# Expert 14's share of expert 15's rows: a product on TensorE in place of a scatter and a gather

## The reference, cut to what matters

```python
def ec_moe(h, router_w, w_gate, w_up, w_down):
    cap = EC_CAPACITY_FACTOR * t // N_EXPERTS          # 2 * 1024 // 16 = 128
    aff = softmax(h @ router_w)
    gate, idx = lax.top_k(swapaxes(aff, 1, 2), cap)     # each expert takes its 128 best tokens
    xs = h[bidx, idx]
    hid = silu(xs @ w_gate) * (xs @ w_up)
    ye = (hid @ w_down) * gate[..., None]
    return zeros_like(h).at[bidx, idx].add(ye)
...
y_lat = ec_moe(h_lat, ...)
x = x + mod_lat[5] * rms_norm(y_lat, norm_g[l, 3])      # the output
```

## Time and profile before

| | us |
|---|---|
| median of three runs | 1482.08 |
| the profiled execution | 1480.8 |
| its span, first to last instruction | 1479.0 |
| TensorE busy | 1302.7 (88%) |
| VectorE busy | 762.0 (52%) |
| ScalarE busy | 479.0 (32%) |
| GpSimd busy | 232.4 (16%) |
| mean granted TensorE clock | 0.948 |

### The profile page before, as it was taken

One profiled execution on the slowest core, in us unless ns is written; L12 is line 12 of the kernel. 1 busy time (PEld: TensorE's weight loads), 2 busy tenths in 40 slices (PEclk: granted clock), 3 DMA queues, 4 the chain that ended last, 5 costly groups with the idle time before them and its releaser, 6 DMA issues.

```text
span 1479.0 us, 13899 instructions
## 1 busy us (share of the span) xinstructions
PE 1302.7 (88%) x5053; PEld 757.3 (51%) x5053; DVE 762.0 (52%) x1079; ACT 479.0 (32%) x1115; POOL 232.4 (16%) x207
## 2 busy tenths in 40 slices
PE   6898998989999999889999969997079999999971
PEld 1444454445545555589989834454034444444430
DVE  1238888978893667577777745563900011001041
ACT  1723542561311222556667623343011110110140
POOL 0001320221000000155554300000010110110121
PEclk9899999999999999999999989998579999999985
DMA  8511544425315110256665654433659999999876
GB/s 305 173 29 50 172 150 143 130 79 180 101 42 157 29 29 20 57 164 172 188 190 188 198 204 154 152 140 109 256 173 356 325 337 341 332 329 337 295 223 147
DMA packets 175274, 264.63 MB, mean 179 GB/s; under 512 B 49069, under 2 KB 91814, under 8 KB 175206
## 3 DMA queue, kind: packets, MB, share of 16 engines
q1 hardware_dynamic: 151286, 204.32, 41.6%
q0 software_dynamic: 14416, 52.96, 12.1%
q10 hardware_dynamic: 9504, 6.45, 1.4%
HBM read 214.47 MB, written 49.22 MB: 178 GB/s over the span
## 4 chain that ended last, share of the span: by engine, by line
PE 59%; DMA 13%; ACT 10%; DVE 10%; issue 4%; SPq 1%; POOL 1%; POOLq 0%; DVEq 0%; ACTq 0%
PE ps L1737 26%; PE ps L1062 12%; PE ps L1081 6%; DMA arena<-g_dram 5%; DMA y_dram<-arena 3%; DMA arena<-zt_dram 2%; PE ps L1026 2%; ACT arena L512 2%; PE ps L1634 2%; PE ps L375 2%; ACT arena L521 1%; PE ps L1688 1%; DVE arena L2046 1%; PE ps L1658 1%; DVE arena L568 1%
## 5 line engine op out<-in xcount | busy, mean ns | idle before, releaser
L1737 PE MATMUL ps<-arena 128*128 128x512 f32 (+1 forms) x1120 | 444.7, 553 | 0.0
L1737 PEld LDWEIGHTS ps<-arena 128*128 128x128 f32 x1120 | 211.9, 192 | 208.5 <-issue 203.3
L1062 PE MATMUL ps<-arena 128*128 128x512 f32 x512 | 228.0, 599 | 1.4 <-ACT arena L1178 1.4
L2046 DVE SCALAR_TENSOR_TENSOR arena<-arena,taps 128x1024 f32<-128x1024 f32 x160 | 213.5, 1334 | 5.7
L1062 PEld LDWEIGHTS ps<-arena 128*128 128x128 f32 x512 | 97.2, 193 | 117.3 <-issue 115.3
L375 PE MATMUL ps<-arena 128*128 128x128 f32 x1080 | 133.7, 279 | 19.1 <-DVE arena L592 15.8
L375 PEld LDWEIGHTS ps<-arena 128*128 128x128 f32 x1080 | 128.9, 193 | 25.6 <-DVE arena L592 19.1
L1341 DVE TENSOR_TENSOR arena<-arena,ps 128x512 f32<-128x512 f32 x16 | 11.0, 687 | 213.4 <-PE ps L1062 213.4
L1026 PE MATMUL ps<-arena 128*128 128x512 f32 x256 | 116.3, 610 | 4.6 <-ACT arena L1127 4.6
L1081 PE MATMUL ps<-arena 128*128 128x512 f32 x256 | 115.6, 606 | 4.9 <-DVE arena L1351 4.9
L1026 PEld LDWEIGHTS ps<-arena 128*128 128x128 f32 x256 | 48.7, 195 | 62.7 <-issue 56.2
(11 more groups left out here) (287 smaller groups left out, 1621.5 us busy)
## 6 DMA issues: line engine op xcount, KB each, us to landing
arena<-exp_w_gate SPq DMA_DIRECT2D x16, 2048.0 KB, 11.3
arena<-exp_w_up SPq DMA_DIRECT2D x16, 2048.0 KB, 8.9
arena<-exp_w_down SPq DMA_DIRECT2D x16, 2048.0 KB, 11.1
arena<-ada_w POOLq DMA_DIRECT2D x16, 1024.0 KB, 6.6
arena<-w_in SPq DMA_DIRECT2D x28, 512.0 KB, 4.0
arena<-ada_w SPq DMA_DIRECT2D x4, 2048.0 KB, 10.6
arena<-x SPq DMA_DIRECT2D x16, 512.0 KB, 8.9
arena<-g_dram SPq DMA_DIRECT2D x16, 512.0 KB, 4.6
```

Source lines behind the costliest of these rows:

```text
L1062: last = mm(ps[gu_bank[s] + j][:], xsT[s][:, k, :], ew[s][j][:, k, :], start=(k == 0), stop=(k == KD - 1))
L1737: last = mm(ps[3 * (m % 2) + gi][:, 0:w], wring[(m + 1) % NW][:, k, :], hT[:, k, o:o + w], start=(k == 0), stop=(k == KD - 1))
L2046: ins = v.scalar_tensor_tensor(accg, cin_l[ci % 2][:, j // 3:j // 3 + GR, j % 3:j % 3 + GW], tp[:, j:j + 1], accg, ALU.mult, ALU.add)
```

## The change

The scatter of expert 14 to `y_dram` goes away, and POOL gathers both row sets from the sums of experts 0 to 13. What expert 14 adds to expert 15's rows is worked out on TensorE. A matrix `same` of 128x128 has a one where row a of expert 14 and row b of expert 15 are the same token, and zeros elsewhere; it is made once, before the first expert, by a transpose of expert 15's broadcast indices and a compare with expert 14's. The product of `same` and `ye` of expert 14, two of 128x512, goes into the banks 2 and 3, in front of expert 15's down product, and VectorE adds it to `yr[1]`.

POOL no longer waits for all tile reads: stores follow as tiles are finished, all eight in a row. N_FIRST becomes 3: ScalarE has three roots in front of its last hidden copy; VectorE does expert 15's hidden product first, then tiles 0 to 2, `ye` of expert 14, `yr[0]`, the wait for TensorE's product and for the rows of expert 15, the add of it, and then tiles 3 to 7.

```diff
-        N_FIRST = 6
+        N_FIRST = 3
...
             pe.wait_ge(sem("route"), 5)
+            tr(ps[1][:, 0:P], pick[:, 1, E_N - 1:E_N].to_broadcast([P, P]), ident[:]).then_inc(sem("affps"), 1)
...
                 if e >= 0:
                     hid_transposed(e)
+                if e == E_N - 1:
+                    pe.wait_ge(sem("ye"), EL + 1)
+                    for h in range(2):
+                        last = mm(ps[gu_bank[EL % 2] + h][:], same, ye[EL % 2][:, h * 512:(h + 1) * 512], start=True, stop=True)
+                    last.then_inc(sem("affps"), 1)
...
+            dve.wait_ge(sem("affps"), 3)
+            v.tensor_scalar(same, ps[1][:, 0:P], pick[:, 1, EL:EL + 1], None, ALU.is_equal)
             for e in range(E_N + 1):
-                if e == E_N - 1:
-                    for t in range(3):
-                        scaled(t, yt[:, t, :]).then_inc(sem("fin"), 1)
...
                 if e == E_N - 1:
-                    for t in range(3, N_FIRST):
+                    for t in range(N_FIRST):
                         scaled(t, yt[:, t, :]).then_inc(sem("fin"), 1)
...
             v.tensor_tensor(yr[0], yr[0], ye[EL % 2], ALU.add).then_inc(sem("rows"), 1)
+            dve.wait_ge(sem("affps"), 4)
+            dve.wait_ge(sem(f"xs_in{EL % NX + 1}"), 16 * (E_N // NX + 1))
+            for h in range(2):
+                hs_ = slice(h * 512, (h + 1) * 512)
+                ins = v.tensor_tensor(yr[1][:, hs_], yr[1][:, hs_], ps[gu_bank[EL % 2] + h][:], ALU.add)
+            link(ins)
             for t in range(N_FIRST, NL):
                 scaled(t, yt[:, t, :]).then_inc(sem("fin"), 1)
             dve.wait_ge(sem("down"), E_N)
-            dve.wait_ge(sem(f"xs_in{EL % NX + 1}"), 16 * (E_N // NX + 1))
...
-            for e in range(E_N - 1):
+            for e in range(EL):
...
-                if e == EL:
-                    pool.wait_ge(sem("y_sc"), 16 * e)
-                    rows_in(yr[0], y_dram, EL, EL % NX)
-                    for i in range(NL // 2):
-                        pool.wait_ge(sem(f"tile_in{i}"), 64)
-                    for i in range(3):
-                        pool.wait_ge(sem(f"xs_in{i}"), 16 * (E_N // NX + 1))
-                    for t in range(N_FIRST):
-                        added(t)
...
-            pool.wait_ge(sem("y_sc"), 16 * (E_N - 1))
-            rows_in(yr[1], y_dram, E_N - 1, EL % NX + 1)
-            for t in range(N_FIRST, NL):
+            pool.wait_ge(sem("y_sc"), 16 * EL)
+            for i in range(LE):
+                rows_in(yr[i], y_dram, EL + i, EL % NX + i)
+            for i in range(LE):
+                pool.wait_ge(sem(f"xs_in{i}"), 16 * (E_N // NX + 1))
+            for t in range(NL):
                 added(t)
             pool.wait_ge(sem("out"), 16 * NL)
```

More of the change, by code:

```diff
@@ L865, in hybrid_block @@
         pick = take(2 * E_N).rearrange("p (r n) -> p r n", r=2)
+        same = take(P)
         idxT = take(E_N).bitcast(U32)
```

## The result

The changed kernel takes 1472.16 us (median of 8 runs, 1470.05 to 1477.19), the kernel before 1480.99 (8 runs, 1478.55 to 1483.15). The ratio is 0.9949 with a 95% interval of 0.9934 to 0.9965: about 7.6 us less, between 5 and 10. The forecast was 1471.9, from a median of 1482.08 that further runs brought down by a microsecond; as a change, 10.2 us were forecast and 8.8 measured by the medians; 10.2 lies just beyond the interval, and the same kernel run again (e9) gave 0.993, about 10.4 us. The profiled execution went from 1480.8 to 1471.23 (span 1479.0 to 1469.4), where 1470.6 had been forecast.

What follows compares the result with a forecast made beforehand. Transfers and their order were taken to bound the tail: DMA sum to 1454.9, plus 2.2 us of cold start gives 1457.1, plus 11.7 for the row scatters a span of 1468.8; forecast median 1471.9 us, range 1467 to 1476.

Steps and rivals of the forecast that it cites:

- The bound and the DMA engines' sum: Tail from 1420.64: transfers bound it; 1.4 us start, 12.9 us plain transfers, 20.0 us adding stores, 1454.9 without pauses.
- the whole cold start: Old stretch from 1434.59: 4.75 us lost to GpSimd's issue, slow first packets and drain; keeping all puts last store at 1459.7.
- The last store at 1457.1: Last output store lands at 1457.1: 1454.9 plus 2.2 us kept of the cold start; bounds 1454.9 to 1459.7.
- The stream hardly breaks: Between stores 2 and 3: store 3 (the fourth) issued at 1439, data flowing by 1441 to 1442, DMA engines busy to about 1442.4.
- rival B: Stream breaks between stores 2 and 3: up to 2.6 us plus 1 of pause, last store near 1460.7, time 1475.5; 24%.
- The end, 11.73 us behind the last store: After the last store the same two row scatters follow, 11.73 us as before, giving a span of 1468.8.
- Covered costs: Expert 15's later down product (over 1446.2 to 1449.9), added transpose and compare cost nothing, hidden by stores ending at 1457.1.
- A: Stores' rate is not the limit: at 405 GB/s last store near 1449, down product sets the end, time 1467; 8%.
- C: Slower: adding stores beside reads keep to 105 GB/s, 4.19 MB need 39.9 us, time 1490; 4%.
- D: Stores end early but expert 15's row sets come late, first ready only at 1467; end stays, time 1482; 4%.

Runs made afterwards that it cites:

- e9: The changed kernel run again, nothing altered: ratio 0.993 to the kernel before; end 47.5 us after the first tile read, against 48.6 in its first profile.
- e5: e2 with its eight output stores writing plainly instead of adding: last store about 27 us after the first tile read, end 42.5 against 46.4.
- e6: e2 with the gather of expert 15's rows issued behind the third store: end 46.8 us after the first tile read, against 46.4.
- e2: Changed kernel with VectorE's wait for the product and its add moved behind tiles 3 to 7: ratio 0.9931 to the kernel before, end 46.4 us after first read.
- e10: The kernel of e2 run again: ratio 0.9922 to the kernel before, median 1469.18 us, end 46.0 us after the first tile read.
- e1: Changed kernel without TensorE's product of expert 14's rows and VectorE's add of it: ratio 0.9928 to the kernel before, end 46.0 us after first read.
- e7: e2 with tiles 5 to 7's old tokens read back, added by VectorE and stored plainly: ratio 0.9923 to the kernel before, end 45.0 us after first read.
- e4: Kernel before with its first six stores following their tiles, expert 14 still scattered: ratio 0.9959 to the kernel before, end 53.7 us after first read.

## Why the prediction was right, point by point

*The bound and the DMA engines' sum:* right, and it is the step that carries the forecast. e5 shows that the adding stores' 2.5 us each are the limit, e6 shows no effect of the order of reads, and e2 and e10 gave, without a break, a last store at 35.5 (mean of two) where the sum from 1420.64 had given 34.3 with nothing lost, 36.5 as forecast and 39.1 with the whole cold start.

*The last store at 1457.1:* it was 1458.66; e9's 36.7 behind the first read would be 1457.4. The 0.3 to 1.6 us are the sum of two errors. The 2.2 us kept of the cold start, a choice, were 1.2 in e2 and e10 (35.5 less 34.3), so one microsecond was spare and took up part of the break of the next point.

*"The stream hardly breaks":* the step that failed. Store 4 was forecast for 1439 and came at 1443.04. Two terms were mis-sized. The product was put at 2 x 0.86 plus 0.5, which is 2.2 us, and took 3.78 (L1100, from 1436.12). The view of its line shows four instructions:

```profile
L1100 PE MATMUL ps<-arena x4: 1061/1061/1222, 1436.1 to 1438.8; 128*128 128x512 f32 x4
```

Two products of 128x512 are four instructions. The rows of before said so too: the down product has eight products in the code and x16 in the earlier trace rows. I had read an instruction as a product, here and in the description of the kernel, where 16 stands for gate, up and down products that are 8 each in the code and 16 instructions each in the trace. And tile 2 was scaled at 1433.46 and not 1431.15, since ScalarE waited 2.2 us for its read, which shared the DMA engines with the gathers. In VectorE's program ye of expert 14 stands behind that tile, so it and the product slid with it. With one gather moved away (e6) it was scaled 1.1 us nearer to the first read than in e2, though two executions of the changed kernel differ by 0.9 there; so how much of it the gathers cost stays open. The sum, 4 us at the fourth store, cost 1.1 to 2.6 us at the end, where rival B had priced the break at 3.6.

*The end, 11.73 us behind the last store:* it was 10.74. That 1 us the other way hid most of the miss before; so the span of 1469.4 beside the forecast's 1468.8 is partly luck: errors of opposite sign made the total look better than its steps. The cause is in the last section.

*Covered costs:* right. The added transpose took 0.48 us at 1076.05 and the compare 0.35, and TensorE still waited 4.12 us for the first gather. The last down product was over at 1447.59 (1439.70 and 7.89), inside the forecast range of 1446.2 to 1449.9, but by two errors again: it began 3.6 us later than forecast and took 7.89 us, not 10.09 or more. The granted clock was 0.74 from 1439.7 to 1443 and 1.00 behind it; in e1, where TensorE had no product to do just ahead of it, it took 9.97. Behind it the second row set was ready at 1454.95, before the last store had landed.

*The rivals:* A fell by e5's contrast, C by the 0.49 MB from 1435 to 1437, where both kinds ran and which their two rates put at 1.9 us, and by 215 GB/s behind them with the engines full (the 345 GB/s from 1431 to 1436 say little on it: 1.61 of the 1.72 MB were reads), D by the wait of 9.46 us for the stores before the first row scatter. B happened in small.

## What to carry to other kernels

Where a tail is made of transfers, add up the bytes at the rate of each kind (an adding store cost twice a plain one here) and ask only whether the stream ever runs dry; moving bytes about inside a full stretch gave nothing here, and a stretch that "looks idle" must be read in the DMA view before something is put there. Don't put a wait for another engine in front of work that feeds the bound when its result is needed only behind it. Count instructions, not products. Compare tails from a common event when the executions begin them microseconds apart, make sure that the edit does not move that event itself (e7), and profile the same kernel twice before you read differences of 2 us.

## What the runs showed of the hardware

An indirect transfer's issue on GpSimd took about 1.0 us when VectorE had no add of two SBUF tiles under way (1.02 at 1458.93 in the changed kernel), and longer when such an add ran beside it. In the kernel before the first row scatter's issue took 1.91 us, with VectorE's add from 1467.33 to 1468.56 beside it, and the transfer landed in 4.27 us against 3.38: these 0.9 us are most of the 1.0 by which the end came out shorter than forecast, for in the changed kernel both adds were over before the last store landed. In e6 one took 2.05 beside an add of 1.23:

```profile
1435.62 1.23 DVE L1363 TENSOR_TENSOR arena<-arena 128x1024 f32<-128x1024 f32 x1
...
1435.72 2.05 POOL L1403 DMA_INDIRECT arena<-y_dram,arena  x1 [0.30 <-issue]
```

In both the add had begun before the issue. In e4, e5 and e7 it began 0.3 to 0.6 us behind the issue, and the issue took 1.17, 1.46 and 1.43 us. Direct stores issued beside VectorE's scalings took 0.85 to 1.00 us. This fits the Trainium skill ("SBUF — State Buffer", section "Who interferes with whom"): VectorE with two SBUF inputs contends with a GpSimd instruction that reads SBUF. The indices of an indirect transfer lie in SBUF in this kernel; that reading them is the reason was not tried. Two things don't fit: the scalings have two SBUF inputs as well, and the same section infers that such an add does not hold up the making of descriptors, where the issues here took up to twice as long.
